# Four of six chunks of the input projection of two layers computed with seven half-size products each

## What is computed

```python
h = rms_norm_2(x, g_mix[layer])
qkv = h @ w_in[layer]                  # 512 x 1024 by 1024 x 3072
qa, ka, va, qb, kb, vb, qc, kc, vc = jnp.split(qkv, cuts, axis=-1)
```

## Time and profile before

| | |
|---|---|
| median of 3 runs | 2241.34 us (2240.23 to 2243.82) |
| the profiled execution's own time | 2240.79 us |
| its span | 2238.9 us |
| PE busy (matmuls) | 2182.8 us, 97% of the span |
| DVE busy | 1367.5 us, 61% |
| POOL busy | 1234.8 us, 55% |
| ACT busy | 856.7 us, 38% |
| chain that ended last | PE 92%, DVE 4% |
| granted TensorE clock, mean | 0.997 of full speed |

### The profile page before, as it was taken

How to read it: one execution, slowest core, us unless ns; L and a number is a source line. 1 busy time by engine, 2 the same in 40 slices (tenths; PEclk the granted TensorE clock), 3 DMA queues, 4 the chain that set the end, 5 groups by cost and what they waited for, 6 DMA issues and landing times.

```text
span 2238.9 us, 31594 instructions
## 1 busy us (share of the span) xinstructions
PE 2182.8 (97%) x11755; PEld 1817.0 (81%) x11755; DVE 1367.5 (61%) x2088; ACT 856.7 (38%) x1766; POOL 1234.8 (55%) x578
## 2 busy tenths in 40 slices
PE   7999999999999999999999999999999999999997
PEld 4788788877899988787787898888786787889885
DVE  6834777554666682435646767677336627777676
ACT  3254663012565600104643555412015635555311
POOL 4756403776477677874016645577773026544673
PEclk9999999999999999999999999999999999999999
DMA  8322102522233343222002222322221002223221
GB/s 327 143 76 94 48 29 90 186 84 93 72 105 107 113 155 113 95 94 76 1 3 92 95 102 87 113 94 94 94 94 57 1 20 94 78 111 114 95 94 57
DMA packets 32769, 206.68 MB, mean 92 GB/s; under 512 B 4080, under 2 KB 4336, under 8 KB 11632
## 3 DMA queue, kind: packets, MB, share of 16 engines
q1 hardware_dynamic: 32192, 200.27, 25.3%
q10 hardware_dynamic: 432, 4.46, 0.5%
HBM read 202.61 MB, written 2.10 MB: 91 GB/s over the span
## 4 chain that ended last, share of the span: by engine, by line
PE 92%; DVE 4%; issue 1%; ACT 1%; POOL 0%; DVEq 0%; DMA 0%; ACTq 0%; SPq 0%; POOLq 0%
PE PS L1005 21%; PE PS L1006 21%; PE PS L1007 21%; PE PS L1403 5%; PE PS L1429 4%; PE PS L1216 3%; PE PS L1217 3%; PE PS L1218 3%; PE PS L1292 2%; PE PS L1294 2%; PE PS L1293 2%; PE PS L1418 2%; DVE ring L2544 1%; PE PS L1019 1%; PE PS L1459 1%
## 5 line engine op out<-in xcount | busy, mean ns | idle before, releaser
L593 POOL TENSOR_TENSOR w_hi<-raw,zero_c 128x512 fp32r<-128x512 f32 (+1 forms) x155 | 352.6, 2291 | 614.5 <-PE PS L1007 611.4
L597 POOL TENSOR_TENSOR w_lo<-raw,w_hi 128x512 fp32r<-128x512 f32 (+1 forms) x155 | 459.9, 2983 | 7.4
L1005 PE MATMUL PS<-b_hi,w_hi 128*128 128x512 f32 x528 | 209.8, 397 | 1.0 <-POOL w_lo L775 1.0
L1007 PE MATMUL PS<-b_hi,w_lo 128*128 128x512 f32 x528 | 209.3, 396 | 0.0
L1006 PE MATMUL PS<-b_lo,w_hi 128*128 128x512 f32 x528 | 209.3, 396 | 0.0
L3055 DVE TENSOR_TENSOR b_lo<-a_all,b_hi 128x512 fp32r<-128x512 f32 x44 | 162.6, 3733 | 49.0 <-ACT b_hi L2229 49.0
L1005 PE MATMUL PS<-f_hi,w_hi 128*128 128x512 f32 x448 | 177.6, 396 | 0.7 <-DVE f_lo L2373 0.7
L1007 PE MATMUL PS<-f_hi,w_lo 128*128 128x512 f32 x448 | 177.6, 397 | 0.0
L1006 PE MATMUL PS<-f_lo,w_hi 128*128 128x512 f32 x448 | 177.6, 396 | 0.0
L1005 PE MATMUL PS<-w_hi,f_hi 128*128 128x512 f32 x384 | 153.0, 399 | 0.0
L1006 PE MATMUL PS<-w_lo,f_hi 128*128 128x512 f32 x384 | 152.1, 396 | 0.0
(11 more groups left out here) (531 smaller groups left out, 6042.4 us busy)
## 6 DMA issues: line engine op xcount, KB each, us to landing
raw<-slabs_dram SPq DMA_DIRECT2D x161, 1024.0 KB, 4.8
aux<-ada_dram SPq DMA_DIRECT2D x18, 512.0 KB, 5.2
ada_first<-ada_dram SPq DMA_DIRECT2D x11, 512.0 KB, 14.0
cmpw<-cmpw_dram ACTq DMA_DIRECT2D x2, 2048.0 KB, 11.5
ada_late<-ada_dram SPq DMA_DIRECT2D x8, 512.0 KB, 3.7
ada_last<-ada_dram SPq DMA_DIRECT2D x8, 512.0 KB, 6.7
xT<-xT_dram SPq DMA_DIRECT2D x1, 2048.0 KB, 8.8
out_dram<-t SPq DMA_DIRECT2D x4, 512.0 KB, 2.7
```

The source lines that it names most:

```text
L593: high = nc.gpsimd.tensor_tensor(w_hi[:, slot, c], raw[:, slot, c], zero[:, 0:c.stop - c.start], ALU.add)
L597: low = nc.gpsimd.tensor_tensor(w_lo[:, slot, c], raw[:, slot, c], w_hi[:, slot, c].bitcast(f32), ALU.subtract)
L1005: nc.tensor.matmul(out, a_hi_, b_hi_, start=start, stop=False)
L1007: return nc.tensor.matmul(out, a_lo_, b_hi_, start=False, stop=stop)
```

## The change

In each of the two layers, chunks 1 to 4 (slabs 2 to 9 of the 12) are computed with seven products each; chunks 0 and 5 stay as they are. A chunk's weights are seen as blocks A11, A12, A21 and A22: the first index says which 256 of its columns, the second which half of the contraction (A11 and A21 lie in its first slab, A12 and A22 in its second). Each is 128 x 1024 elements in memory. A product is 24 matmuls with 256 moving columns. PE's order in a chunk is M1, M2, M4, M5, M6, M3, M7, with weights A11, A12, A22, S1, S2, S4, S3. M1, M2 and M3 use `f_hi` and `f_lo`; M4 to M7 use four sums of activation blocks, `ys_hi` and `ys_lo`, formed once per layer from `in_form`, an unrounded copy of x times the gain.

- ACT: eight operations for `in_form`, four for `ys_hi` (`form_high`), seven weight high parts of 128 x 1024 per chunk (`high`), four times two copies of 128 x 256 out of PSUM (`snap`); the last chunk's high parts (`last_high`).
- POOL: one activation sum (x3) and one `ys_lo`; low parts of M1, M2, M4 and M7; the last chunk's low parts. It makes no high part of slabs 2 to 11 any more. It releases a chunk's two slabs to SP (`release`) when all four weight sums are made and its own low parts are done.
- DVE: three activation sums and three `ys_lo`; four weight sums per chunk; low parts of M5, M6 and M3; the other halves of the results are added from PSUM (`take`, two operations of 128 x 256 each); the ropes.
- The mean of the squares is computed by PE after the first slab of chunk 0 and no longer two blocks into the second. Semaphores `early_hi`, `early_low` and `tok_root` are merged into others.

The diff, cut to its core:

```diff
+IN_ORDER = ("M1", "M2", "M4", "M5", "M6", "M3", "M7")
+FORM = {"M4": 3, "M5": 2, "M6": 0, "M7": 1}
...
+
+                x3 = in_sums[FORM["M7"]]
+                pool.wait_ge(in_formed, KD * (ct.layer + 1))
+                nc.gpsimd.tensor_tensor(x3[:], in_form[:, 4:8, 256:512], in_form[:, 0:4, 256:512], ALU.subtract
+                                        ).then_inc(xt_pool, 1)
+                def release(n):
+                    pool.wait_ge(w_summed, ct.sums + 4 * n + 4)
+                    pool.drain().then_inc(slab_split, 1)
+
+                for n in range(IN_HALVED):
+                    low(n, "M1").then_inc(op_pool_low, 1)
+                    if n > 0:
+                        release(n)
+                    low(n, "M2").then_inc(op_pool_low, 1)
+                    low(n, "M4").then_inc(op_pool_low, 1)
+                    if n == 0:
+                        release(n)
+                    release(n)
+                    if n == 0:
+                        pool.wait_ge(xt_hi, 4 * ct.layer + 4)
+                        nc.gpsimd.tensor_tensor(ys_lo[FORM["M7"]][:], x3[:], ys_hi[FORM["M7"]][:].bitcast(f32),
+                                                ALU.subtract)
+                    low(n, "M7").then_inc(op_pool_low, 1)
+                for s in (0, 1):
+                    slot = (ct.slot + s) % 2
+                    for half in (0, 1):
+                        c = slice(1024 * half, 1024 * half + 1024)
+                        pool.wait_ge(op_hi, ct.highs + 7 * IN_HALVED + 2 * s + half + 1)
...
+                def product(n, what):
+                    if what in ("M1", "M2", "M4", "M7"):
+                        pe.wait_ge(op_pool_low, ct.low(n, what))
+                    else:
+                        pe.wait_ge(op_dve_low, ct.low(n, what))
+                    if n == 0 and what in ("M4", "M5", "M6"):
+                        pe.wait_ge(xt_lo, 3 * layer + {"M4": 1, "M5": 2, "M6": 3}[what])
+                    if what == "M1" and n > 0:
+                        pe.wait_ge(banks_drained, at_.drain + n)
+                    if what == "M2":
+                        if n == 0:
+                            pe.wait_ge(tok_sum, layer + 1)
+                        else:
+                            pe.wait_ge(c11_taken, ct.taken + n)
+                    if what == "M4":
+                        if n == 0:
+                            pe.wait_ge(banks_drained, at_.drain + 1)
+                        else:
+                            pe.wait_ge(snapped, ct.snap(n - 1, "M4"))
+                    if what == "M5":
+                        if n == 0:
+                            pe.wait_ge(banks_drained, at_.drain + 1)
+                        else:
+                            pe.wait_ge(c12_taken, ct.taken + n)
+                    if what in ("M6", "M3", "M7"):
+                        pe.wait_ge(snapped, ct.snap(n, {"M6": "M1", "M3": "M5", "M7": "M6"}[what]))
...
+                high(0, "M1")
+                high(0, "M2")
+                form_high("M4", xt_sum, 3 * layer + 3)
+                form_high("M5", xt_sum, 3 * layer + 3)
                 act.wait_ge(tok_sum, at_.mixes)
-                A(tok, tok, ACT.Sqrt, bias=eps_c).then_inc(tok_root, 1)
-
-            def evacuate_one(dst, c, bank0):
+                A(tok, tok, ACT.Sqrt, bias=eps_c).then_inc(root_ready, 1)
+                form_high("M6", xt_sum, 3 * layer + 3)
+                act.wait_ge(slab_used, ct.base + 2)
+                high(0, "M4")
+                form_high("M7", xt_pool, layer + 1)
...
+                    snap(n, "M4", 1, 0)
+                    high(n, "M7")
+                    act.wait_ge(op_used, ct.used(n, "M5"))
+                    snap(n, "M5", 1, 1)
+                    if final:
+                        last_high(0, 0)
+                    else:
+                        high(n + 1, "M1")
+                    act.wait_ge(op_used, ct.used(n, "M6"))
+                    snap(n, "M6", 0, 1)
+                    if final:
+                        last_high(0, 1)
+                    else:
+                        high(n + 1, "M2")
+                    act.wait_ge(op_used, ct.used(n, "M3"))
+                    if final:
+                        last_high(1, 0)
+                    else:
+                        high(n + 1, "M4")
+                    act.wait_ge(slab_used, ct.slab(n, 1) + 1)
+                    if final:
+                        last_high(1, 1)
+                    else:
+                        high(n + 1, "M5")
+                at_.slab += N_IN2 - 2
 
...
                 if gained is not None:
+                    b11, b12, b21, b22 = (in_form[:, k:k + 4, q:q + 256] for k in (0, 4) for q in (0, 256))
+                    x2, _, x1, x4 = in_sums
+
+                    def form_low(what):
+                        V.tensor_tensor(ys_lo[FORM[what]][:], in_sums[FORM[what]][:], ys_hi[FORM[what]][:].bitcast(f32),
+                                        ALU.subtract).then_inc(xt_lo, 1)
+
+                    dve.wait_ge(in_formed, KD * (at_.mixes + 1))
+                    then(V.tensor_tensor(x1[:], b12, b11, ALU.subtract).then_inc(xt_sum, 1))
+                    then(V.tensor_tensor(x2[:], b22, x1[:], ALU.subtract).then_inc(xt_sum, 1))
+                    V.tensor_tensor(x4[:], b21, x2[:], ALU.subtract).then_inc(xt_sum, 1)
+                    dve.wait_ge(xt_hi, 4 * at_.mixes + 1)
+                    form_low("M4")
+                    dve.wait_ge(xt_hi, 4 * at_.mixes + 2)
+                    form_low("M5")
...
+
+                def sums(n, last):
+                    blocks = in_blocks(ct)
+                    if last:
+                        if n > 0:
+                            dve.wait_ge(op_pool_low, ct.low(n - 1, "M7"))
+                        V.tensor_tensor(in_s3, blocks["A11"], blocks["A21"], ALU.subtract).then_inc(w_summed, 1)
+                        return
+                    for m in (ct.slab(n, 0), ct.slab(n, 1)):
+                        dve.wait_ge(slab_loaded[m % 2], 16 * (m // 2) + 16)
+                    dve.drain()
+                    then(V.tensor_tensor(in_s1, blocks["A21"], blocks["A22"], ALU.add).then_inc(w_summed, 1))
+                    then(V.tensor_tensor(in_s2, in_s1, blocks["A11"], ALU.subtract).then_inc(w_summed, 1))
+                    if n == 0:
+                        dve.wait_ge(xt_pool, layer + 1)
+                    V.tensor_tensor(in_s4[:], blocks["A12"], in_s2, ALU.subtract).then_inc(w_summed, 1)
+
+                def low(n, what):
+                    dve.wait_ge(op_hi, ct.high(n, what))
+                    V.tensor_tensor(in_ring(w_lo, ct, n, what), in_operand(ct, what),
+                                    in_ring(w_hi, ct, n, what).bitcast(f32), ALU.subtract).then_inc(op_dve_low, 1)
+
+                def take(n, what, r, q):
+                    for i in (0, 1):
+                        to = in_part(n, r, q, i)
+                        last = V.scalar_tensor_tensor(out=to, in0=PS[:, in_bank(n, what), 256 * i:256 * i + 256],
+                                                      scalar=tok[:, 2 * q + i:2 * q + i + 1], in1=to, op0=ALU.mult,
+                                                      op1=ALU.add)
+                    return last
+
+                sums(0, False)
+                sums(0, True)
+                for n in range(IN_HALVED):
+                    low(n, "M5")
+                    if n == 0:
+                        dve.wait_ge(banks_drained, drained + 1)
+                    rope(n)
+                    low(n, "M6")
+                    dve.wait_ge(op_used, ct.used(n, "M2"))
+                    dve.wait_ge(snapped, ct.snap(n, "M1"))
+                    take(n, "M2", 0, 0).then_inc(c11_taken, 1)
+                    low(n, "M3")
+                    if n + 1 < IN_HALVED:
+                        sums(n + 1, False)
+                        sums(n + 1, True)
+                    dve.wait_ge(op_used, ct.used(n, "M3"))
+                    dve.wait_ge(snapped, ct.snap(n, "M6"))
+                    take(n, "M3", 0, 1).then_inc(c12_taken, 1)
+                    dve.wait_ge(slab_used, ct.slab(n, 1) + 1)
+                    take(n, "M7", 1, 1).then_inc(c22_taken, 1)
+                    take(n, "M7", 1, 0).then_inc(c21_taken, 1)
+                    dve.drain().then_inc(banks_drained, 1)
+                rope(IN_HALVED)
```

226 lines of the change are left out of this document (166 added, 60 removed).

## The result

| | before | changed |
|---|---|---|
| median of seven runs each | 2243.82 us (2240.23 to 2248.13) | 2252.00 us (2249.34 to 2256.58) |
| profiled execution | 2240.79 us | 2250.59 us (span 2248.8) |

The changed kernel takes 1.0041 of the time of before, with a 95% interval of 1.0029 to 1.0052: slower by 0.4%. The forecast of 2247.5 us had the sign, and the range of 2231 to 2258 us holds the time. Of the 4.5 us between forecast and time, 2.5 us are the median of before itself, which stood at 2241.34 us when the forecast was made.

What follows compares the result with a forecast made beforehand. PE was taken to bound both input stages. Per layer -10.5 us of matmuls, +11.4 of idle time at the start and +2.2 of clock gave +3.1, +6.2 in all: 2247.5 us against 2241.3, range 2231 to 2258.

Steps and rivals of the forecast that it cites:

- PE is the bound and the steady chunks have no wait: Both input stages: PE always busy; chunks behind the start run at 19.8 us without idle time.
- VectorE bounds every chunk: Rival, input chunks: VectorE's 13.5 us plus waits for POOL make 23.1 us; 2274 us, milder form 2255; 6% together.
- The gain of 10.5 us per layer: Input chunks with seven products: 2.63 us saved per chunk, 10.5 us per layer, 21.0 us in all.
- 168 of them, 19.77 us: Each seven-product chunk: 7 x 24 matmuls of 256 columns at 0.1177 us each, against 22.40 us before.
- The walk through the start: Chunk 1 of each layer: PE idle 1.7 us ahead of M4, 2.2 ahead of M5, 7.5 ahead of M6.
- The sum of 11.4: Start of each layer's input stage: PE's three idle times together, 11.4 us, more than the 10.5 gained.
- The clock, 2.2 us per layer: Behind M6's wait in chunk 1: the granted clock falls, costing 2.2 us a layer, bounds 0 and 4.
- the clock stays up: Rival, start of the stages: idle time as walked but no lasting clock fall; +1.8 us, 2243 us, no change; 23%.
- The sum.: Per layer: -10.5 gain, +11.4 idle time, +2.2 clock, so +3.1 us; +6.2 us in all.
- The rival of better cover: Start of the stages: POOL's low parts fall behind the rope, M6 waits 2.7 us, clock holds; 2233.5 us; 25%.
- Nothing is in the way: Rival, start of the stages: no waits, all 21 us come, 2220 us; 3% within the better-cover rival.

Runs made afterwards that it cites:

- e7: The changed kernel with the operands of the half-size products swapped (weights stationary, 256 tokens moving; outputs not the reference's): 2250.85 us, 1.0035 of before.
- e5: The changed kernel with 16 idle matmuls of 128x256 on PE ahead of M6 of chunk 1: 2248.61 us, 1.0023 of before.
- e2: The changed kernel with GpSimd waiting for the rope of chunk 0 before its ys_lo and low part of M7: 2244.02 us, 0.9997 of before.
- e8: The changed kernel with chunk 0's rope late, the start reordered, and GpSimd's low part of M2 ahead of the slab release: 2231.82 us, 0.9956 of before.

## Why the prediction was right, point by point

- **PE is the bound and the steady chunks have no wait: right.** VectorE's 13.5 us and GpSimd's turns did not hold PE up in any chunk behind the start. The rival "VectorE bounds every chunk" fell.
- **The gain of 10.5 us per layer: too large, the term that was mis-sized.** The step is "168 of them, 19.77 us". It took the up projection's 0.1177 us, where the weights are the stationary operand. Here the tokens are, and a matmul takes 0.1200 us. The gain is 4 x (22.40 - 20.17) = 8.9 us, 3.2 us less in both layers together. e7 shows that the roles make a difference, all of it in the first layer and half in the second.
- **The walk through the start: right in each step.** The forecast counted from where PE could have started, so its waits are compared from start to start: M4 1.7 us forecast, 1.33 and 1.05 measured; M5 2.2 against 2.34 and 2.35; M6 7.5 against 7.62 and 7.26. The sum of 11.4 was 11.29 and 10.66. The rope was to have three operations of over 2 us and to end at 943.1; it had three, and ended at 943.37.
- **The clock, 2.2 us per layer: right.** From M6's start on the changed kernel lost 2.71 and 2.42 us; e5 got back 2.5 and 2.2 of them. The rival "the clock stays up" fell, and so did its 2243 us. That the same M5 wait would bring the clock down in some executions and not in others was not in the forecast.
- **The sum.** In the first layer -8.9 + 11.29 + 2.71 = +5.1 us, in the second -8.9 + 10.66 + 2.42 = +4.2 us, where I had +3.1 for each. The stages grew by 5.02 and 4.12 us, so the three terms account for them. The misses are +1.6 us in the gain, -0.1 and -0.7 in the waits, +0.5 and +0.2 in the clock: the sign does not rest on errors that cancelled. Both layers make 9.1 of the 9.8 us between the two profiled executions; the other 0.7 lie outside the stages.
- **The rival of better cover** named a right lever: e2 is nearly that rival, with GpSimd's operations behind the rope. I had given it a wait of 2.7 us and no fall of the clock. It had 3.36 and 1.96 us and a fall in both layers, since one operation of GpSimd still got ahead of M6's low part, and M5's wait brought the clock down in the second. So it stayed at 2244 us instead of 2233.5. I had not looked at the rope's place as the cheaper cure.
- **"Nothing is in the way", 2220 us** could not be had: with the start almost free of waits, e8 stands at 2232, and at 0.1200 us per matmul the whole gain is 17.8 us, so 2226 from before's 2243.8.

## What to carry to other kernels

When a stage's products get shorter, walk its first chunk instruction by instruction. In the steady state the queues have a lead; at the start they have none, and here that cost 14.0 and 13.1 us, more than the whole gain of 8.9. Look in each in-order queue for what nobody needs yet (a rotation of finished data, a release) and stands ahead of what the bounding engine waits for; moving one such block was worth 16 us here. Then look for the next one, because the bounding engine, now earlier, will reach a wait that its lateness had covered.
